# Four layer boundaries: the first tokens' x turned before the last late weight piece, and six late pieces in every one of the four stages

## The chip, the cores and the metric

The kernel runs on one core of a Trainium2 chip. The metric is device time in microseconds (us), median of several runs. Engines: TensorE (PE in the profile, its weight loads PEld), VectorE (DVE), ScalarE (ACT), GpSimd (POOL) and SyncE (SP, which issues the weight loads).

## What is computed

256 tokens of 1024 features go through a long chain of layers: a first block of depth two (gated feed-forwards, an mLSTM mixer, a differential attention, gated per-layer embeddings), a second block (attention beside a state-space mixer, then a product-key expert layer), and a third block (gated recurrence beside forgetting attention, then a feed-forward). Each sublayer begins by norming x and ends by adding its normed result to x. The four boundaries of this case lie between a projection and the next sublayer:

```python
h = swiglu(rms_norm(x, g[0]), w_ffn_in[layer, 0], w_ffn_out[layer, 0])   # f00, f10
x = x + 0.5 * rms_norm(h, g[1])
h = rms_norm(x, g[2])                                                     # boundary f00 -> ml
h = mlstm_mixer(h, ...)            # layer 0: ml; layer 1: df, diff_attention
x = x + rms_norm(h, g[3])
h = swiglu(rms_norm(x, g[4]), w_ffn_in[layer, 1], w_ffn_out[layer, 1])    # boundaries ml -> f01, df -> f11
...
x = x + rms_norm_3(mix_out, mix_norm_post[layer])
h = rms_norm_3(x, ffn_norm_pre[layer])                                    # boundary m3 -> f3
```

Everything is in fp32 accuracy: each weight and each activation is split in a high and a low half, and three of the four products are made.

## The kernel before

**Stages.** f00, ml, f01, p0, f10, df, f11, p1, m2, pr, m3 and f3 run in this order. Each ends in a `down` product, which is accumulated over weight pieces in four PSUM banks: two for the first 128 tokens (j = 0), two for the second (j = 1).

**Weight pieces.** SP loads chunks of 1 MB into three slots. ACT makes the high half of each piece of 128x1024 (`high_to`, L2589), DVE the low half (`low_to`, L1375). The halves live in a ring of four buffers, or aside in free parts of a large array (`ASIDE`, `FOLLOW`). A planner's loop in `Program` says how many pieces are made ahead (`upto`), and both engines make them in a fixed place of their own program. A load into a slot waits for the low halves of the chunk before in that slot.

**Late pieces.** `down` (L654) runs over KT pieces, 22 in a feed-forward and 8 in ml, df and m3. Most are used for both token halves at once, twelve matmuls of L622 each. The last `LATE[key]` pieces are kept: first all of them for j = 0 (six matmuls each), then all of them for j = 1, so that the first tokens' banks fill early. LATE is 6 for f00 and 5 for ml, df and m3.

**The boundary.** When its banks are full, `residual` (DVE L1434 weighting, L1447 sum, L1461 moment; ACT L2630 squares, L2637 squares of x; POOL L1265 the inverse root) gives the new x, and L2645 (ACT) and L1467 (DVE) its normed halves. TensorE turns it by transposes (`turn_half`, L505). ACT scales the eight turned tiles of a token half into the high part (L2614) and DVE makes the low part (L1413); the code calls both `enter`. Then `four` (L559, matmuls L573) makes the next stage's first four pieces, 24 matmuls for the first tokens, then the second turn, then 24 for the second tokens. Before the change the order on TensorE is: late pieces j = 0, late pieces j = 1, turn of j = 0, `four` for j = 0, turn of j = 1, `four` for j = 1. On ACT the squares of j = 1 come before `enter` of j = 0; on DVE all of the weighting and sum of j = 1 comes before it.

**df's down.** `before(t)` puts the end of the differential attention between its pieces on TensorE: heads' probabilities are turned (L855), the values' products made (L881 to L883), and the heads' outputs turned in pairs (L905). Pieces 0 and 1 run before the parts of t = 2, piece 2 runs between those and the parts of t = 3; pieces 3 to 7 are the late ones. On DVE and ACT the halves of the next pieces stand between the attention's parts too; the copy of a head's values is L1850, its norming L1863.

Of the kernel before, what the change touches and what calls it, by code (L numbers as in the profile page):

```python
# [298 lines left out]
class Program:  # L299
# [150 lines left out]
    def gb(self, slot):  # L450
# [11 lines left out]
LATE = {"f00": 6, "ml": 5, "f01": 5, "p0": 8, "f10": 5, "df": 5, "f11": 5, "p1": 8, "m2": 3, "pr": 4, "m3": 5, "f3": 3}  # L462
ASIDE = {"f00": (23552, 13312, 15360, 17408, 19456, 21504), "ml": (20608, 22656, 0, 4096, 6144),
# [8 lines left out]
          "pr": (4096, 6144), "m3": (10240, 22656)}  # L472
# [3 lines left out]
def tensor_engine(k):  # L476
# [177 lines left out]
    def down(key, KT, act, ready, ring=32, before=nothing):  # L654
# [15 lines left out]
        for j in range(2):  # L670
            for t, n, hi, lo in kept:
                ins = products(t, n, hi, lo, (j,))
                if j:
                    ins.then_inc(k.piece_read, 1)
            if j == 0:
                filled((key, "o", 0), ins)
            else:
                k.full[key, "o", 1] = k.piece_read, n + 1
# [52 lines left out]
    def ffn(key, prev, third=nothing):  # L731
        turn_half(key + ".x", prev, 0)
        second = lambda: turn_half(key + ".x", prev, 1)
        if key == "f00":
            second()
        gated(key, 22, turned_x(key + ".x"), None if key == "f00" else second, third)
        down(key, 22, k.pair(0, 22), hidden(key))
# [13 lines left out]
    def mlstm(prev):  # L751
        turn_half("ml.x", prev, 0)
# [71 lines left out]
        down("ml", 8, k.pair(14336, 8), out_halves("ml"))  # L824
# [33 lines left out]
    def diff(prev, kx, kv_ready):  # L858
# [72 lines left out]
        down("df", 8, k.pair(4096, 8), turned("df.o"), before=before)  # L931
# [217 lines left out]
    def mix3(prev):  # L1149
# [45 lines left out]
        down("m3", 8, k.pair(0, 8), out_halves("m3.o"))  # L1195

    def ffn3(prev):
        turn_half("f3.x", prev, 0)
# [4 lines left out]
    ffn("f00", "in")  # L1203
# [156 lines left out]
def vector_engine(k):  # L1360
# [57 lines left out]
    def residual(key, src, banks, row, factor, more, arrive, pre=nothing):  # L1418
# [4 lines left out]
        enter = into[key] if more else nothing  # L1423
# [58 lines left out]
        x_low(0)  # L1482
        if not banks:
# [19 lines left out]
        if not tokens_next:  # L1503
            if banks:
# [8 lines left out]
        if banks and not tokens_next:  # L1513
            enter(0, range(4, 8))
# [808 lines left out]
    def mix3(prev):  # L2323
# [106 lines left out]
        mg, tt, mx = k.ar(14336, 8, 256), k.ar(21632, 2, 2, 256), k.pair(0, 8)  # L2430
# [141 lines left out]
def scalar_engine(k):  # L2572
# [45 lines left out]
    def residual(key, src, banks, row, factor, more, arrive, pre=nothing, mid=nothing):  # L2618
# [37 lines left out]
        if banks:  # L2656
            x_high(0)
            square(1, 0)
            square(1, 1)
            mid(0)  # L2660
            enter(0)
# [539 lines left out]
    def mix3(prev):  # L3201
# [86 lines left out]
        tt, mx = k.ar(21632, 2, 2, 256), k.pair(0, 8)  # L3288
# [266 lines left out]
```

## Time and profile before

| | us |
|---|---|
| median of 3 runs | 2874.62 (2874.25 to 2874.62) |
| the profiled execution, device time | 2875.41 |
| its span from first to last instruction | 2873.6 |
| TensorE busy | 2818.5 (98%) |
| DVE busy | 1952.3 (68%) |
| ACT busy | 1636.2 (57%) |
| mean granted TensorE clock | 0.995 |

A matmul's time in the trace runs from its issue to its modelled end, and successive ones overlap, so a busy TensorE is not one at its peak. What counts at a boundary is the start of each group of instructions on each engine. A timeline line gives the start of a group, the time from its first start to its last end, the engine, the source line and operation, output and inputs, the count, and in brackets the idle time of the engine before it with what ended it.

### The profile page before, as it was taken

To read this page: it belongs to the slowest core of one execution; us is meant where nothing else is said; L and a number is where in the kernel's file an instruction comes from. 1 tells how busy PE (TensorE), PEld (TensorE's weight loads), DVE (VectorE), ACT (ScalarE), POOL (GpSimd) and SP (SyncE) were. 2 spreads that over 40 slices of the span, in tenths; PEclk is the share of its full clock that TensorE was granted. 3 is DMA by queue.
4 is the path that set the end of the run, shared out by engine and by line. 5 is a ranking of instruction groups with operands and counts; after the bars stand their busy time and mean duration, and the time that the engine had idled before them with its cause. 6 is when DMAs were issued, how large, how long until landed. Compare 5 with 4: busy or idle time off the path is not lost.

```text
span 2873.6 us, 44340 instructions
## 1 busy us (share of the span) xinstructions
PE 2818.5 (98%) x17826; PEld 2544.8 (89%) x17826; DVE 1952.3 (68%) x3367; ACT 1636.2 (57%) x2802; POOL 342.4 (12%) x310
## 2 busy tenths in 40 slices
PE   8999999999989999999999999999999999999999
PEld 7889888788978877899999999999888889999997
DVE  6657765676676667768864898677555566756775
ACT  5545654755655564556655445777454555755663
POOL 0000000000010002000001444896000000000000
PEclk9999999999999999999999999999999999999999
DMA  6654556456435555445365554334555564536454
GB/s 213 198 170 161 178 198 214 132 194 223 142 117 168 204 175 179 132 138 183 89 184 170 189 177 162 133 133 148 196 197 192 190 233 129 185 106 213 136 195 150
DMA packets 304539, 490.32 MB, mean 171 GB/s; under 512 B 10880, under 2 KB 236544, under 8 KB 295632
## 3 DMA queue, kind: packets, MB, share of 16 engines
q1 hardware_dynamic: 303200, 480.09, 50.6%
q0 software_dynamic: 1136, 7.41, 0.7%
q8 instruction: 142, 2.33, 0.3%
q14 instruction: 61, 0.50, 0.1%
HBM read 485.37 MB, written 2.10 MB: 170 GB/s over the span
## 4 chain that ended last, share of the span: by engine, by line
PE 89%; DVE 7%; ACT 2%; DMA 1%; issue 1%; POOL 0%; SPq 0%; DVEq 0%; POOLq 0%; ACTq 0%
PE ps L622 30%; PE ps L556 11%; PE ps L552 11%; PE ps L553 11%; PE ps L701 10%; PE ps L700 5%; PE ps L573 2%; PE ps L1130 2%; DVE halves L1375 2%; PE ps L1165 1%; PE ps L505 1%; DVE AR L2234 1%; DVE R L1375 1%; PE ps L855 0%; DMA raw<-in_w_ffn_in 0%
## 5 line engine op out<-in xcount | busy, mean ns | idle before, releaser
L2589 ACT ACTIVATE halves<-raw 128x1024 fp32r<-128x1024 f32 (+1 forms) x842 | 878.6, 1052 | 681.6 <-PE ps L622 330.7
L1375 DVE TENSOR_TENSOR halves<-raw,halves 128x1024 fp32r<-128x1024 f32 (+1 forms) x806 | 964.3, 1218 | 223.3 <-ACT halves L2589 220.6
L552 PE MATMUL ps<-XX,halves 128*128 128x256 f32 (+1 forms) x2360 | 586.7, 286 | 0.0
L553 PE MATMUL ps<-XX,halves 128*128 128x256 f32 (+1 forms) x2360 | 578.3, 283 | 0.0
L622 PE MATMUL ps<-halves,XX 128*128 128x512 f32 x2256 | 525.0, 393 | 5.5 <-DVE XX L1413 2.8
L622 PEld LDWEIGHTS ps<-halves,XX 128*128 128x128 f32 x2256 | 424.4, 189 | 96.9 <-DVE XX L1413 5.2
L552 PEld LDWEIGHTS ps<-XX,halves 128*128 128x128 f32 (+1 forms) x2360 | 451.5, 191 | 0.8
L553 PEld LDWEIGHTS ps<-XX,halves 128*128 128x128 f32 (+1 forms) x2360 | 452.0, 192 | 0.3
L556 PE MATMUL ps<-XX,halves 128*128 128x256 f32 (+1 forms) x2360 | 331.5, 283 | 0.7 <-DVE halves L1375 0.7
L622 PE MATMUL ps<-halves,R 128*128 128x512 f32 x1404 | 322.3, 391 | 0.0
L701 PE MATMUL ps<-XX,halves 128*128 128x512 f32 x1264 | 317.8, 393 | 2.2 <-DVE XX L1413 2.2
L622 PEld LDWEIGHTS ps<-halves,R 128*128 128x128 f32 x1404 | 264.3, 189 | 54.6
L556 PEld LDWEIGHTS ps<-XX,halves 128*128 128x128 f32 (+1 forms) x2360 | 304.3, 192 | 1.2 <-DVE halves L1375 1.1
L701 PEld LDWEIGHTS ps<-XX,halves 128*128 128x128 f32 x1264 | 227.4, 189 | 43.1 <-issue 2.5
L1265 POOL TENSOR_TENSOR st<-st 128x1 f32<-128x1 f32 x44 | 27.9, 635 | 1507.7 <-DVE st L1440 1305.7
L700 PEld LDWEIGHTS ps<-XX,halves 128*128 128x128 f32 x1264 | 172.4, 190 | 13.5 <-issue 1.3
L700 PE MATMUL ps<-XX,halves 128*128 128x256 f32 x1264 | 176.3, 282 | 1.0 <-DVE halves L1375 1.0
L1390 DVE TENSOR_TENSOR XX<-AR,XX 128x256 fp32r<-128x256 f32 x128 | 54.2, 425 | 142.8 <-ACT XX L3194 142.8
L1345 POOL TENSOR_SCALAR raw<-iota,xsel 128x128 f32<-128x128 f32 x128 | 136.7, 1074 | 37.5 <-PE ps L1130 23.2
L1596 DVE TENSOR_TENSOR AR<-AR,ps 128x256 f32<-128x256 f32 x164 | 68.6, 421 | 83.1 <-ACT AR L2755 83.1
L2755 ACT ACTIVATE AR<-ps 128x256 f32<-128x256 f32 x164 | 61.3, 376 | 88.7 <-PE ps L701 88.7
L1270 POOL TENSOR_TENSOR halves<-raw,halves 128x1024 fp32r<-128x1024 f32 x36 | 91.5, 2540 | 157.6 <-ACT halves L2589 157.6
(365 smaller groups left out, 3505.1 us busy)
## 6 DMA issues: line engine op xcount, KB each, us to landing
raw<-in_w_ffn_in SPq DMA_DIRECT2D x88, 1024.0 KB, 5.1
raw<-in_w_in SPq DMA_DIRECT2D x74, 1024.0 KB, 5.3
raw<-in_uT SPq DMA_DIRECT2D x64, 1024.0 KB, 4.9
raw<-in_peer_v SPq DMA_DIRECT2D x64, 1024.0 KB, 4.9
raw<-in_w_ffn_out SPq DMA_DIRECT2D x44, 1024.0 KB, 4.9
raw<-in_w_up SPq DMA_DIRECT2D x24, 1024.0 KB, 5.8
raw<-in_mlstm_w_in SPq DMA_DIRECT2D x12, 1024.0 KB, 5.4
raw<-in_w_down SPq DMA_DIRECT2D x12, 1024.0 KB, 4.9
```

The source lines that it names most:

```text
L552: mm(o[:, ts], hi[:, q, 0:M], xh[:, k0 + q, ts], start=first and q == 0, stop=False)
L553: mm(o[:, ts], hi[:, q, 0:M], xl[:, k0 + q, ts], start=False, stop=False)
L556: ins = mm(o[:, ts], lo[:, q, 0:M], xh[:, k0 + q, ts], start=False, stop=last and q == a - 1)
L622: ins = mm(ps[:, bs[j * (width // 512) + h], :], xv[:, k0 + t, j * 128:(j + 1) * 128], wv[:, t, h * 512:(h + 1) * 512], start=first and q ...
L700: mm(o[:, 0:256], lo[:, p, :], X[0][:, p, :], start=False, stop=False)
L701: ins = mm(o.rearrange("p (h t) -> p h t", t=256), hi[:, q, :], k.XX[:, :, q, :], start=q == 0, stop=q == 7)
L1270: nc.gpsimd.tensor_tensor(lo, src, hi.bitcast(F32), ALU.subtract).then_inc(k.lo_pool, 1)
L1345: nc.gpsimd.tensor_scalar(OA[:, g % 2, q, :], k.iota[:], ih1[:, 4 * g + q:4 * g + q + 1], gw[:, 4 * g + q:4 * g + q + 1], ALU.is_equal, AL ...
L1375: te.tensor_tensor(lo, src, hi.bitcast(F32), ALU.subtract).then_inc(k.lo_made, 1)
L1596: te.tensor_tensor(dst, dst, o[:, 0:256], ALU.add) \
L2589: act(hi, src, ACT.Copy).then_inc(k.hi_made, 1)
L2755: act((sg if a_ == "g" else hb)[:, f // 2 % 2, g, :], ps[:, k.wide_banks(f).of(tile), 256:512], ACT.Copy) \
```

## The change

- `ml`, `df` and `m3` get a sixth late piece, with a place aside for it; m3's last places move, and m3's scratch tile `tt` moves to make room.
- For f00, ml, df and m3 (`TURNED_EARLY`) the turn of the first tokens' x is issued inside `down`, before the last late piece of j = 1, and no longer at the start of the next stage.
- On ACT `enter` of the first tokens (all eight tiles) comes before the second tokens' squares. On DVE its tiles 0 to 3 come before the second tokens' weighting, tiles 4 to 7 after their sum and before their moment.

```diff
-LATE = {"f00": 6, "ml": 5, "f01": 5, "p0": 8, "f10": 5, "df": 5, "f11": 5, "p1": 8, "m2": 3, "pr": 4, "m3": 5, "f3": 3}
+LATE = {"f00": 6, "ml": 6, "f01": 5, "p0": 8, "f10": 5, "df": 6, "f11": 5, "p1": 8, "m2": 3, "pr": 4, "m3": 6, "f3": 3}
-ASIDE = {..., "ml": (20608, 22656, 0, 4096, 6144),
+ASIDE = {..., "ml": (20608, 22656, 0, 4096, 6144, 11264),
-         "f10": (13312, 20480, 22528, 24576, 0), "df": (13312, 15360, 17408, 24576, 0),
+         "f10": (13312, 20480, 22528, 24576, 0), "df": (13312, 15360, 17408, 24576, 0, 19456),
-         "pr": (0, 2048, 4096, 6144), "m3": (4096, 6144, 8192, 10240, 22656)}
+         "pr": (0, 2048, 4096, 6144), "m3": (4096, 6144, 8192, 10240, 22528, 24576)}
+TURNED_EARLY = ("f00", "ml", "df", "m3")
...
     def down(key, KT, act, ready, ring=32, before=nothing, turn_next=nothing):
...
         for j in range(2):
             for t, n, hi, lo in kept:
+                if j and t == KT - 1:
+                    turn_next()
                 ins = products(t, n, hi, lo, (j,))
...
-        turn_half(key + ".x", prev, 0)
+        if prev not in TURNED_EARLY:
+            turn_half(key + ".x", prev, 0)
...
-        down("ml", 8, k.pair(14336, 8), out_halves("ml"))
+        down("ml", 8, k.pair(14336, 8), out_halves("ml"), turn_next=lambda: turn_half("f01.x", "ml", 0))
...
@@ vector_engine, residual
         x_low(0)
+        if key in TURNED_EARLY:
+            enter(0, range(4))
...
         if not tokens_next:
-            if banks:
+            if key in TURNED_EARLY:
+                enter(0, range(4, 8))
+            elif banks:
                 enter(0, range(4))
...
-        if banks and not tokens_next:
+        if banks and not tokens_next and key not in TURNED_EARLY:
             enter(0, range(4, 8))
...
@@ mix3
-        mg, tt, mx = k.ar(14336, 8, 256), k.ar(21632, 2, 2, 256), k.pair(0, 8)
+        mg, tt, mx = k.ar(14336, 8, 256), k.ar(16384, 2, 2, 256), k.pair(0, 8)
...
@@ scalar_engine, residual
             x_high(0)
+            if key in TURNED_EARLY:
+                enter(0)
             square(1, 0)
             square(1, 1)
             mid(0)
-            enter(0)
+            if key not in TURNED_EARLY:
+                enter(0)
```

The downs of f00, df and m3 get their `turn_next` in the same way, and the turns at the start of ml and f3 are taken out.

## Rows read from the trace of the kernel before

**Rows 1.** The page, chain that ended last: shares of the span by engine.

```profile
PE 89%; DVE 7%; ACT 2%; DMA 1%; issue 1%; POOL 0%; SPq 0%; DVEq 0%; POOLq 0%; ACTq 0%
```

**Rows 2.** Timeline, boundary f00: start us, us, engine, line, operation, xcount, idle before.

```profile
197.77 0.72 ACT L2645 ACTIVATE AR<-AR,st 128x512 f32<-128x512 f32 x1 [0.91 <-POOL st L1265]
...
200.33 1.03 PE L505 MATMUL ps<-ident,AR 128*128 128x128 f32 x8
...
200.53 1.41 DVE L1434 TENSOR_TENSOR AR<-ps,AR 128x512 f32<-128x512 f32 x2 [2.27 <-PE ps L622]
...
202.35 5.85 PE L573 MATMUL ps<-halves,XX 128*128 128x512 f32 x24 [0.98 <-ACT XX L2614]
...
206.13 0.73 ACT L2645 ACTIVATE AR<-AR,st 128x512 f32<-128x512 f32 x1 [0.91 <-POOL st L1265]
...
208.04 1.03 PE L505 MATMUL ps<-ident,AR 128*128 128x128 f32 x8
```

**Rows 3.** Timeline, boundary ml.

```profile
299.82 13.31 PE L622 MATMUL ps<-R,R 128*128 128x512 f32 x58
...
305.37 2.36 DVE L1375 TENSOR_TENSOR halves<-raw,halves 128x1024 fp32r<-128x1024 f32 x2 [1.09 <-ACT halves L2589]
...
307.65 1.28 DVE L1434 TENSOR_TENSOR AR<-ps,AR 128x512 f32<-128x512 f32 x2
...
313.06 0.72 ACT L2645 ACTIVATE AR<-AR,st 128x512 f32<-128x512 f32 x1 [0.92 <-POOL st L1265]
...
313.93 1.06 PE L505 MATMUL ps<-ident,AR 128*128 128x128 f32 x8 [0.80 <-ACT AR L2645]
...
321.05 1.03 PE L505 MATMUL ps<-ident,AR 128*128 128x128 f32 x8
```

**Rows 4.** Timeline, boundary m3.

```profile
2651.85 2.36 DVE L1375 TENSOR_TENSOR halves<-raw,halves 128x1024 fp32r<-128x1024 f32 x2 [0.73 <-ACT halves L2589]
...
2654.13 1.28 DVE L1434 TENSOR_TENSOR AR<-ps,AR 128x512 f32<-128x512 f32 x2
...
2659.53 0.72 ACT L2645 ACTIVATE AR<-AR,st 128x512 f32<-128x512 f32 x1 [0.91 <-POOL st L1265]
...
2660.40 1.06 PE L505 MATMUL ps<-ident,AR 128*128 128x128 f32 x8 [0.57 <-ACT AR L2645]
...
2667.50 1.03 PE L505 MATMUL ps<-ident,AR 128*128 128x128 f32 x8
```

**Rows 5.** Timeline, boundary df.

```profile
849.84 1.41 DVE L1434 TENSOR_TENSOR AR<-ps,AR 128x512 f32<-128x512 f32 x2 [2.81 <-PE ps L622]
...
855.26 0.73 ACT L2645 ACTIVATE AR<-AR,st 128x512 f32<-128x512 f32 x1 [0.92 <-POOL st L1265]
...
856.45 1.03 PE L505 MATMUL ps<-ident,AR 128*128 128x128 f32 x8
...
864.20 1.03 PE L505 MATMUL ps<-ident,AR 128*128 128x128 f32 x8
864.84 2.17 ACT L2614 ACTIVATE XX<-ps,cols 128x128 fp32r<-128x128 f32 x8 [1.87 <-PE ps L505]
...
866.01 2.16 DVE L1413 SCALAR_TENSOR_TENSOR XX<-ps,cols,XX 128x128 fp32r<-128x128 f32 x8 [3.00 <-ACT XX L2614]
```

**Rows 6.** Timeline of TensorE, the end of df's attention.

```profile
827.44 4.39 PE L622 MATMUL ps<-halves,R 128*128 128x512 f32 x12
...
840.25 0.69 PE L905 MATMUL ps<-ident,AR 128*128 128x128 f32 x2 [7.31 <-DVE AR L1863]
```

**Rows 7.** Chain of work that ended last, same stretch: start us, us, what.

```profile
831.35 5.06 DMA raw<-in_w_ffn_in
...
838.74 0.34 DVE AR L1850
```

**Rows 8.** Stretches: us, busy PE, PEld, DVE, ACT, POOL (x), PEclk, DMA share, GB/s.

```profile
540.30:543.70 3.40, 1.70 (x6) 0.75 (x5) 2.61 (x8) 2.00 (x5) 0.55 (x1) 1.00 0.55 188
543.70:547.10 3.40, 3.24 (x12) 2.96 (x13) 0.91 (x4) 2.19 (x10) 0.00 (x0) 0.50 0.00 0
...
840.60:844.00 3.40, 3.18 (x10) 2.37 (x10) 2.52 (x7) 2.12 (x4) 0.18 (x1) 0.50 0.33 103
```

More of the change, by code:

```diff
@@ L460 @@
               "pr": 128, "m3": 8, "f3": 24}
-LATE = {"f00": 6, "ml": 5, "f01": 5, "p0": 8, "f10": 5, "df": 5, "f11": 5, "p1": 8, "m2": 3, "pr": 4, "m3": 5, "f3": 3}
-ASIDE = {"f00": (23552, 13312, 15360, 17408, 19456, 21504), "ml": (20608, 22656, 0, 4096, 6144),
+LATE = {"f00": 6, "ml": 6, "f01": 5, "p0": 8, "f10": 5, "df": 6, "f11": 5, "p1": 8, "m2": 3, "pr": 4, "m3": 6, "f3": 3}
+ASIDE = {"f00": (23552, 13312, 15360, 17408, 19456, 21504), "ml": (20608, 22656, 0, 4096, 6144, 11264),
          "f01": (14848, 16896, 18944, 20992, 23040), "p0": (16384, 18432, 20480, 22528),
[1 row of a table removed]
[1 row of a table added]
          "f11": (14848, 16896, 18944, 20992, 23040), "p1": (16384, 18432, 20480, 22528),
          "m2": (0, 12288, 23552),
[1 row of a table removed]
[1 row of a table added]
+TURNED_EARLY = ("f00", "ml", "df", "m3")
 FOLLOW = {"f00": (15360, 21504), "ml": (20608, 22656), "p0": (16384, 18432), "df": (15360, 17408), "m2": (0, 12288),
-          "pr": (4096, 6144), "m3": (10240, 22656)}
+          "pr": (4096, 6144), "m3": (10240, 22528)}
 FACTOR = {"f00": 0.5, "f01": 0.5, "f10": 0.5, "f11": 0.5}
@@ L652, in tokens, with down @@
                 k.full[key, s0, j] = k.piece_read, n + 1
-    def down(key, KT, act, ready, ring=32, before=nothing):
+    def down(key, KT, act, ready, ring=32, before=nothing, turn_next=nothing):
         bs = [aux.take(pe, (key, "o", i)) for i in range(4)]
@@ L729, in out_halves, with ffn @@
         return lambda t: [s["out_lo"].need((key, t - t % 2))]
-    def ffn(key, prev, third=nothing):
-        turn_half(key + ".x", prev, 0)
+    def ffn(key, prev, third=nothing, turn_next=nothing):
+        if prev not in TURNED_EARLY:
+            turn_half(key + ".x", prev, 0)
         second = lambda: turn_half(key + ".x", prev, 1)
@@ L736, in ffn @@
         gated(key, 22, turned_x(key + ".x"), None if key == "f00" else second, third)
-        down(key, 22, k.pair(0, 22), hidden(key))
+        down(key, 22, k.pair(0, 22), hidden(key), turn_next=turn_next)
     def turn_kv(_):
@@ L751, in mlstm @@
     def mlstm(prev):
-        turn_half("ml.x", prev, 0)
         rx = turned_x("ml.x")
@@ L929, in before @@
                 out_pair(6)
-        down("df", 8, k.pair(4096, 8), turned("df.o"), before=before)
+        down("df", 8, k.pair(4096, 8), turned("df.o"), before=before, turn_next=lambda: turn_half("f11.x", "df", 0))
     def attend(key, score, vv, yt, E_, dT, value_need, expd):
@@ L1194, in mix3 @@
         features("m3.pb", 8, k.pair(17536, 8), lambda c: [aux.gone(("m3", "y", c - c % 2))])
-        down("m3", 8, k.pair(0, 8), out_halves("m3.o"))
+        down("m3", 8, k.pair(0, 8), out_halves("m3.o"), turn_next=lambda: turn_half("f3.x", "m3", 0))
     def ffn3(prev):
-        turn_half("f3.x", prev, 0)
         gated("f3", 24, turned_x("f3.x"), lambda: turn_half("f3.x", prev, 1))
@@ L1202, in tensor_engine @@
     pe.wait_ge(*s["vec"].need("constants"))
-    ffn("f00", "in")
+    ffn("f00", "in", turn_next=lambda: turn_half("ml.x", "f00", 0))
     mlstm("f00")
@@ L3287, in mix3 @@
         yT, E_ = k.pair(17536, 8), k.ar(23680, 2, 384)
-        tt, mx = k.ar(21632, 2, 2, 256), k.pair(0, 8)
+        tt, mx = k.ar(16384, 2, 2, 256), k.pair(0, 8)
         gt = (k.ar(2048, 8, 256), k.ar(12288, 8, 256))
```

## The prediction, made before the change was run

> **What bounds the kernel now.** I read the page's chain of work first, then the timeline of the four boundaries that the diff touches. TensorE is the bound: 89% of the chain is its own work [rows 1], so time is won or lost only where TensorE stands idle or is delayed. At a boundary the reader should see three things: when TensorE finishes the down product, when the first tokens' x is normed (L2645, ACT), and when the second tokens' x is turned (the second run of L505). The second is the new wait to watch, because TensorE goes on only when both turns are done.
>
> At f00 the first turn runs 200.33, the four pieces' first half (L573) starts at 202.35 after 0.98 idle, and the second turn starts at 208.04 although the second x was normed at 206.13 + 0.73 = 206.86 [rows 2]. So there is 1.18 us of slack in the second tokens' tail. At ml the run of L622 ends at 299.82 + 13.31 = 313.13, the first turn waits until 313.93 for L2645, and the second is at 321.05 [rows 3]. m3 is the same picture (2660.40 and 2667.50) [rows 4]. At df the first turn waits for nothing (x normed at 855.99, turn at 856.45), the second is at 864.20 [rows 5].
>
> **The change, in units.** One matmul of L622 takes (13.31 - 0.39) / 57 = 0.227 us from start to start (58 in 13.31, each 0.39 long) [rows 3]. A late piece has six for each token half: 1.36 us. Eight turning transposes take 1.03 us in all, and the next matmul can follow after 0.87 (1.03 less the overlap of the last, seven steps of about 0.11) [rows 2].
>
> **Part 1, the turn moved ahead of the last late piece.** It wants to start 1.36 us before the old end of L622. Call its start T. Then the last piece runs T + 0.87 to T + 2.23, and the four pieces' first half follows at once: ACT takes the eight turned tiles from T + 0.64 to T + 2.81 (864.84 - 864.20, and 2.17 long) [rows 5], just ahead of TensorE. The idle 0.98 before L573 is gone. That is the gain, about 1.1 us where T isn't late.
>
> **Part 2, the second tokens' tail.** Their banks are full at T + 2.4, but ACT takes their squares only after the eight tiles, T + 2.8, and DVE starts their weighting after four low halves: it can begin at T + 1.81 (866.01 - 864.20), four of the eight take about 1.12, less 0.08 of overlap with the next: T + 2.85 [rows 5]. From the weighting to the second norm it is 206.13 - 200.53 = 5.60 [rows 2], then 0.73 for the norm and 0.15 to the turn (313.06 + 0.72 = 313.78, turn at 313.93) [rows 3]. Second turn: T + 2.85 + 5.60 + 0.73 + 0.15 = **T + 9.33**. TensorE has reached it at T + 2.23 + 24 x 0.227 = T + 7.7, so a new wait of 1.6 us takes the place of the old gap. For df's first tokens, with nothing beside them, the same stretch took 855.26 - 849.84 = 5.42 [rows 5]; that is the lower bound, T + 9.15, and I keep 5.60, since four low halves still sit between the sum and the moment on DVE. Queued behind the waiting turn on TensorE: the other token half, then everything. Nothing hides it.
>
> **Part 3, the sixth late piece and whether T is late.** T is the later of "old end less 1.36" and "x normed plus 0.15".
> - f00 has six late pieces already. The wanted T is 200.33 - 1.36 = 198.97, x is normed at 197.77 + 0.72 = 198.49 [rows 2]. T = 198.97, second turn 208.30 against 208.04: **+0.26**.
> - ml: the wanted T is 313.13 - 1.36 = 311.77. The sixth late piece fills the first tokens' banks 1.36 earlier, at 305.0 instead of 306.3. But DVE is making low halves of the next four weight pieces until 305.37 + 2.36 = 307.73 and starts the weighting at 307.65 [rows 3]; these come at the arrival of weights, in DVE's program order, and the diff leaves the order alone: by the planner's loop the pieces made ahead at each late piece are the same from the eighth last on. So x is normed at 313.78 as before, and T stays 313.93, 2.16 us after TensorE wants it. Second turn 323.26 against 321.05: **+2.21**.
> - m3: weighting at 2654.13, at the end of the same kind of low halves; T stays 2660.40; second turn 2669.73 against 2667.50: **+2.23** [rows 4].
> - df: the weighting starts with the full banks (849.84), so T = 856.45 - 1.36 = 855.09 does move with them; 864.42 against 864.20: **+0.22** [rows 5].
>
> **Part 4, df's third piece.** With five late pieces, piece 2's twelve matmuls stand between the attention's last parts: 4.39 us from 827.44 [rows 6]. After them TensorE waits 7.31 us, until 840.25, for head 6 and 7. That wait is not TensorE's doing: the chain goes through a weight load from 831.35 to 836.41, its halves, and then the copy of head 7's values at 838.74 [rows 7], which ACT and DVE have queued behind the halves of the next pieces. With six late pieces the twelve matmuls leave this cover. The wait grows and ends at the same time; the twelve come after it: 12 x 0.227 = **+2.72**. Bounds: 0 if the load came correspondingly sooner, 4.39 if they ran at the half clock throughout. The clock is 0.50 just after 840.60 [rows 8] in any case, so the work that follows loses the same there; I take 2.72.
>
> The tiles' new places (tt, the sixth aside piece) cost nothing that a row shows: no instruction is added. No DMA is moved; SP's loads wait for low halves, which don't move before the norms.
>
> **Sum.** 0.26 + 2.21 + 0.22 + 2.23 + 2.72 = **7.6 us**. The profiled execution took 2875.41 (span 2873.6) and would take 2883.0; it is 0.8 above the median of 2874.62, which becomes **2882.2**. About 0.2%, or 5.7 us, is what a measurement of this kernel can tell from no change.
>
> **Clock.** A stretch in which TensorE was busy 1.70 of 3.40 us was followed by one at 0.50, which is 1.2 GHz [rows 8]. The new waits at ml and m3 (2.16 and 1.93, then 1.6) are of that size, so the half clock may follow. If it falls on the four pieces' first half it costs 1.7 and the second wait of 1.6 hides nearly all; if it falls later it costs up to 1.7 a boundary. The Trainium skill (TensorE: Matmul & The Clock Gate, HAM oscillation) makes trouble only of idle gaps longer than these; by it this is 0, by the row up to 3.4 for the two. I leave it out of the sum and keep it in the range.
>
> The Trainium skill (ScalarE: Activation LUTs, What ACT_TABLE_LOAD costs) gives by its formula an estimate of 0.29 us for each of ACT's eight back-to-back tiles; row 864.84 has 0.27. By the page the tail would be some 0.2 us longer at each boundary, 8.4 in all instead of 7.6.
>
> **Rivals.**
> 1. *The first norm follows the banks* (faster side of slower). If ml's and m3's weighting starts 1.36 sooner, T does too: 7.6 - 2 x 1.36 = 4.9, **2879.5**. For it: the chain really starts from full banks at f00 and df. Against it: 307.65 touches the end of L1375 [rows 3]. The same time comes out if df's load comes sooner by the twelve matmuls (7.6 - 2.7). 17%.
> 2. *It works as meant: faster.* One mechanism: both token halves' x are ready when TensorE wants them, so each boundary gives back its idle time before L573: 1.1 at f00 and df, 1.3 at ml, 1.1 at m3, sum 4.6, **2870.0**. It decides at T + 7.7: the second tail would have to be 1.6 us shorter than its row, T on time at ml and m3, and df's twelve matmuls free. 9%.
> 3. *Half clock beyond the cover* at ml, m3 or after df's longer wait: 2 x 1.7 more, **2885.6**. 12%.
> 4. The forecast, 2880.5 to 2884: 62%.
>
> **Range and chances.** The range takes in the forecast, rival 1 and most of rival 3 down to the tail's lower bound: 2878.0 to 2886.0; outside are rival 2 and the ends. Slower by over 0.2% needs 2880.4: forecast nearly whole and rival 3, 0.68; within 0.2%: rival 1 and the forecast's lower end, 0.23; faster 0.09.
>
> **What would show it.** f00: no idle before L573, second turn near 9.3 after the first with an idle of about 1.6 before it. ml and m3: 2 us idle before the first turn, with six matmuls of L622 behind it, and L1434 starting still at the end of L1375. df: the wait before L905 grows from 7.3 to about 10 and ends on the same load; 72 matmuls of late pieces after it instead of 60. Wrong if at ml L1434 starts with the first tokens' banks, if the tail from the first to the second turn is under 8 us, or if L905's wait ends sooner.

## The result and the profile after

| | before | after |
|---|---|---|
| median of 12 runs each, us | 2873.78 (2871.08 to 2875.45) | 2880.15 (2876.90 to 2884.95) |
| the profiled execution, device time | 2875.41 | 2878.57 |
| its span | 2873.6 | 2876.8 |
| mean granted TensorE clock | 0.995 | 0.995 |

The ratio is 1.0026, with an interval of 1.0018 to 1.0034: 0.0026 x 2873.78 = 7.5 us slower (5.2 to 9.8); the medians differ by 6.4. The change makes the kernel slower, by about what was forecast (7.6). One execution of late_only, an experiment below, took 3973.31 us at a mean granted clock of 0.654 and is in no ratio.

Two words are used throughout. The *tail* of a boundary is the time from the start of the first tokens' turn to the start of the second tokens' turn. A load's *landing* is the moment at which ACT, idle until then for this load, starts on it.

Line numbers of after lie 1 to 6 higher: L505 is L506, L573 is L574, L622 is L623, L905 is L908, L1375 is L1377, L1434 is L1436, L1863 is L1869, L2589 is L2595, L2614 is L2620, L2645 is L2651. I read the four boundaries first, as before.

**f00**, timeline of after: start us, us, engine, line, operation, xcount, idle before.

```profile
198.98 1.03 PE L506 MATMUL ps<-ident,AR 128*128 128x128 f32 x8
199.62 2.18 ACT L2620 ACTIVATE XX<-ps,cols 128x128 fp32r<-128x128 f32 x8 [1.11 <-PE ps L506]
199.77 1.63 PE L623 MATMUL ps<-R,R 128*128 128x512 f32 x6
...
201.24 5.91 PE L574 MATMUL ps<-halves,XX 128*128 128x512 f32 x24
201.84 1.28 DVE L1436 TENSOR_TENSOR AR<-ps,AR 128x512 f32<-128x512 f32 x2
```

The turn starts at 198.98, the six matmuls of the last late piece follow it, and the four pieces start 2.26 us after the turn with no idle: the 0.98 before L573 in [rows 2] is gone, as the change means it. What it gets in return stands in the weighting of the second tokens, 201.84, which is 2.86 behind the turn, and in the second turn at 208.25 (208.04 before).

**ml and m3**, two stretches of the timeline of after:

```profile
303.79 2.01 ACT L2595 ACTIVATE halves<-raw 128x1024 fp32r<-128x1024 f32 x2 [1.00 <-DMA raw<-in_w_ffn_in]
304.89 2.36 DVE L1377 TENSOR_TENSOR halves<-raw,halves 128x1024 fp32r<-128x1024 f32 x2 [0.65 <-ACT halves L2595]
...
307.17 1.28 DVE L1436 TENSOR_TENSOR AR<-ps,AR 128x512 f32<-128x512 f32 x2
...
313.45 1.06 PE L506 MATMUL ps<-ident,AR 128*128 128x128 f32 x8 [0.38 <-ACT AR L2651]
...
322.75 1.06 PE L506 MATMUL ps<-ident,AR 128*128 128x128 f32 x8 [1.09 <-ACT AR L2651]
...
2651.65 2.01 ACT L2595 ACTIVATE halves<-raw 128x1024 fp32r<-128x1024 f32 x2 [2.42 <-DMA raw<-in_w_up]
...
2655.02 1.28 DVE L1436 TENSOR_TENSOR AR<-ps,AR 128x512 f32<-128x512 f32 x2
...
2661.30 1.06 PE L506 MATMUL ps<-ident,AR 128*128 128x128 f32 x8 [1.66 <-ACT AR L2651]
...
2670.60 1.06 PE L506 MATMUL ps<-ident,AR 128*128 128x128 f32 x8 [1.10 <-ACT AR L2651]
```

The second turn is 9.30 behind the first in both (7.12 and 7.10 in [rows 3, 4]), and TensorE waits for the norm of the second tokens' x, where before the norm was done when TensorE came to it. The weighting still starts at the end of the low halves of L1377 (304.89 + 2.36 = 307.25).

**df**, timeline of TensorE in after:

```profile
841.12 0.69 PE L908 MATMUL ps<-ident,AR 128*128 128x128 f32 x2 [9.05 <-DVE AR L1869]
...
842.54 17.44 PE L623 MATMUL ps<-R,R 128*128 128x512 f32 x66
...
859.82 1.04 PE L506 MATMUL ps<-ident,AR 128*128 128x128 f32 x8
...
869.10 1.06 PE L506 MATMUL ps<-ident,AR 128*128 128x128 f32 x8 [1.10 <-ACT AR L2651]
```

The wait before heads 6 and 7 is 9.05 us (7.31 in [rows 6]), and now 66 matmuls follow it before the turn. What ends it is a weight load, in the chain of work that ended last: start us, us, what.

```profile
832.25 5.03 DMA raw<-in_w_ffn_in
...
837.30 1.07 ACT halves L2595
...
838.39 1.23 DVE halves L1377
839.62 0.34 DVE AR L1856
```

It is the chain of [rows 7], link by link. The link ahead of the load is a low half on DVE (L1377, 831.09 and 1.14 long; 830.19 and 1.15 in before): it frees the slot, and the load is issued. So the end of the wait hangs on DVE's order as well as on the 5.03 us of the transfer.

**The four boundaries in one table.** From the first matmul of `down` to the second turn, in us, each worked out from two starts in the timeline; the same for every kernel of the experiments, so that what differs elsewhere between two executions is kept out. The last column has the tails:

| kernel | f00 | ml | df | m3 | sum | first to second turn |
|---|---|---|---|---|---|---|
| before | 67.57 | 29.95 | 48.09 | 29.61 | 175.2 | 7.70, 7.12, 7.76, 7.10 |
| after | 67.77 | 31.40 | 52.10 | 33.14 | 184.4 | 9.27, 9.30, 9.28, 9.30 |
| df_five_late | 67.78 | 33.00 | 49.23 | 33.05 | 183.1 | 9.27 to 9.31 |
| late_only | 67.60 | 30.65 | 50.77 | 30.85 | 179.9 | 7.74, 7.18, 7.76, 7.31 |
| turn_only | 67.78 | 31.38 | 49.74 | 31.81 | 180.7 | 9.27 to 9.31 |
| old_order_act_dve | 68.51 | 33.44 | 52.13 | 33.57 | 187.6 | 9.99 to 10.02 |
| lazy_late_waits | 67.78 | 31.54 | 52.24 | 32.35 | 183.9 | |
| early_norm_changed | 67.78 | 32.45 | 51.96 | 32.68 | 184.9 | 9.27, 10.21, 9.27, 10.21 |
| fill_df_wait | 67.57 | 29.61 | 46.66 | 31.16 | 175.0 | 7.70, 7.55, 7.74, 7.10 |
| fill_df_wait_early_norm | 67.61 | 29.76 | 46.22 | 30.74 | 174.3 | ml 7.88, m3 8.19 |
| fill_df_wait_more | 67.59 | 29.61 | 44.63 | 30.07 | 171.9 | ml 7.52, m3 7.10 |

After has 9.2 us more than before at the boundaries, but its profiled execution is only 3.2 longer. The other 6 lie elsewhere, and nothing in the traces ties them to the change: in the execution of before TensorE ran at half clock in stretches of 3.4 us near 543.7 [rows 8], 1079.6 and 1089.8 and for 6.8 us near 1386.8, 17.1 in all; in that of after for 3.4 us near 1093.0. Half of the difference, 6.8, is the most that this can be worth. So one execution of each can't be compared by its end; the boundaries can, and so can 12 runs.

### The profile page after: what moved, and what is told of

It is laid out like the page before. It is cut to its first block, busy times and chain, and to the rows that moved or that the text cites. A ratio compares the mean times of both kernels' runs of the same rounds, so it can differ in the third digit from the quotient of the medians.

```text
span 2876.8 us, 44338 instructions
## 1 busy us (share of the span) xinstructions
PE 2814.6 (98%) x17826; PEld 2539.8 (88%) x17826; DVE 1951.7 (68%) x3367; ACT 1637.6 (57%) x2802; POOL 342.4 (12%) x310
## 4 chain that ended last, share of the span: by engine, by line
PE 88%; DVE 7%; ACT 2%; DMA 1%; issue 1%; POOL 1%; SPq 0%; DVEq 0%; POOLq 0%; ACTq 0%
PE ps L623 30%; PE ps L557 11%; PE ps L553 11%; PE ps L554 11%; PE ps L704 10%; PE ps L703 5%; PE ps L1133 2%; DVE halves L1377 2%; PE ps L574 2%; PE ps L1168 1%; DVE XX L1415 1%; PE ps L506 1%; DVE R L1377 1%; POOL st L1267 1%; DVE AR L2240 1%
## 5 line engine op out<-in xcount | busy, mean ns | idle before, releaser
L2595 ACT ACTIVATE halves<-raw 128x1024 fp32r<-128x1024 f32 (+1 forms) x839 | 875.5, 1052 | 678.4 <-PE ps L623 329.5
L1377 DVE TENSOR_TENSOR halves<-raw,halves 128x1024 fp32r<-128x1024 f32 (+1 forms) x803 | 960.7, 1217 | 222.7 <-ACT halves L2595 219.6
L623 PE MATMUL ps<-halves,XX 128*128 128x512 f32 x2256 | 522.5, 392 | 5.5 <-DVE XX L1415 2.9
L623 PEld LDWEIGHTS ps<-halves,XX 128*128 128x128 f32 x2256 | 422.5, 188 | 96.1 <-DVE XX L1415 5.2
L623 PE MATMUL ps<-halves,R 128*128 128x512 f32 x1368 | 312.5, 389 | 0.0
L623 PEld LDWEIGHTS ps<-halves,R 128*128 128x128 f32 x1368 | 256.4, 188 | 53.0
L623 PE MATMUL ps<-R,R 128*128 128x512 f32 x504 | 119.1, 396 | 2.1 <-ACT R L2595 2.1
L623 PEld LDWEIGHTS ps<-R,R 128*128 128x128 f32 x504 | 95.7, 191 | 22.8 <-ACT R L2595 2.9
```

The source lines that it names most:

```text
L623: ins = mm(ps[:, bs[j * (width // 512) + h], :], xv[:, k0 + t, j * 128:(j + 1) * 128], wv[:, t, h * 512:(h + 1) * 512], start=first and q ...
L1377: te.tensor_tensor(lo, src, hi.bitcast(F32), ALU.subtract).then_inc(k.lo_made, 1)
L2595: act(hi, src, ACT.Copy).then_inc(k.hi_made, 1)
```

## The experiments

Two questions. Which of the two parts costs what: the turn with its order, or the sixth late piece? And was each term's reason the one given? The theory is the forecast's: the second tokens' tail of 9.3 (against 7.1 at ml and m3), and df's twelve matmuls out of the cover of a wait whose end is fixed. The rival theories are that the first norm follows the banks (so that the sixth piece gives something back at ml and m3), and that the turn alone would be a gain.

**df_five_late.** After, with df's sixth late piece undone.

```diff
-LATE = {..., "df": 6, ...}
+LATE = {..., "df": 5, ...}
-"df": (13312, 15360, 17408, 24576, 0, 19456)
+"df": (13312, 15360, 17408, 24576, 0)
```

> The changed kernel, but with df's five late pieces back (piece 2's twelve matmuls again between the attention's last parts). Theory A (piece 2 was free cover for a wait that ends on a weight load): TensorE's wait before head 6 and 7 is turned goes from 9.05 us back to about 7.3 us and ends on the same load; the run of late pieces after it is 60 matmuls, not 72; df gives back 2.7 us and up to 1.7 of half clock, so 2.7 to 4.4 us less than the changed kernel. But its first norm then comes 1.1 us after TensorE wants the turn, so the second turn is about 1.3 us later than in the kernel before at df. Against the kernel before: +3.5 to +5. Theory B (the early turn is what costs at df): no more than 1 us against the changed kernel.

Measured: 2878.75, ratio to before 1.0023 (1.0015 to 1.0032), that is +6.6. (The expectation added its own terms wrongly: 0.26, 2.2, 1.3 and 2.2 make 6.0, not 3.5 to 5.) At df it gave back 52.10 - 49.23 = 2.9, for an expected 2.7, and the wait shrank to what twelve matmuls, partly at half clock, leave of it. Two more things are in this 2.9: the norm came 0.89 after the turn's place (second row below), and less of the late run stood at half clock than in after. By the times it gave back only 7.5 - 6.6 = 0.9, with intervals that overlap nearly whole, so the 2.9 is the trace's and not shown by the times. TensorE in df_five_late:

```profile
843.26 0.69 PE L908 MATMUL ps<-ident,AR 128*128 128x128 f32 x2 [7.36 <-DVE AR L1869]
...
858.97 1.06 PE L506 MATMUL ps<-ident,AR 128*128 128x128 f32 x8 [0.89 <-ACT AR L2651]
```

ml, which this edit doesn't touch, took 33.00 instead of 31.40. That led to the reading of the loads below.

**late_only.** Before, with six late pieces and their places, and the old turn and order.

```diff
-LATE = {... "ml": 5, ... "df": 5, ... "m3": 5, ...}
+LATE = {... "ml": 6, ... "df": 6, ... "m3": 6, ...}
```

(with the diff's ASIDE, FOLLOW and `tt`)

> The kernel before with six late pieces in ml, df and m3 (and the new places), but each first turn where it was and the old order on ACT and DVE. Theory A: df alone costs 2.7 to 4.4 us; ml nothing (TensorE waits for the last late pieces' high halves, 0.8 us, but waited for the norm anyway); m3 0.8 us, because its 1.3 us wait for the high halves ends the late run after the norm. Sum +3.5 to +5. Theory B (early turn costs, late pieces are free): within 1 us of the kernel before.

Measured: 2874.77, ratio 1.0011 (1.0003 to 1.0020), that is +3.2, for an expected 3.5 to 5. The boundaries give +4.7, of which df is +2.68: the twelve matmuls (2.72). The run of late matmuls after the wait is 72 long. TensorE in late_only:

```profile
840.12 0.69 PE L905 MATMUL ps<-ident,AR 128*128 128x128 f32 x2 [9.02 <-DVE AR L1863]
...
841.54 17.68 PE L622 MATMUL ps<-R,R 128*128 128x512 f32 x72
```

At ml and m3 the sixth piece gives nothing back: +0.70 and +1.24, where the rival wanted the banks' 1.36 earlier norm to show. What is new there is a wait inside the run, for high halves. It does not end the late run after the norm, as was expected of m3 (TensorE still waits 0.27 for the norm there):

```profile
2642.47 16.58 PE L622 MATMUL ps<-R,R 128*128 128x512 f32 x72 [1.06 <-ACT R L2589]
```

**turn_only.** After, with LATE, ASIDE, FOLLOW and `tt` as before: the early turn and the new order alone.

```diff
-LATE = {... "ml": 6, ... "df": 6, ... "m3": 6, ...}
+LATE = {... "ml": 5, ... "df": 5, ... "m3": 5, ...}
```

> The kernel before with the four first turns ahead of the last late piece and the new order on ACT and DVE, but five late pieces in ml, df and m3. Theory A: from first to second turn 9.3 us at every boundary, so f00 +0.2, ml +2.2, m3 +2.2 (first turns at the time of the norm, as before), df +1.3 (its norm comes 1.1 us late for the wanted turn); sum +6. No 0.8 and 1.3 us waits of L622-type products for high halves at ml and m3, the wait at df 7.3 us. Theory B (the sixth piece is what costs, the early turn gives back the idle second before the four pieces): faster than the kernel before by 3 to 4 us.

Measured: 2876.86, ratio 1.0015 (1.0007 to 1.0024), boundaries +5.5: 0.21, 1.43, 1.65 and 2.20. The turn alone loses at every one of the four; the theory by which it is a gain is refuted. df costs more than the forecast's 0.22, which was for six late pieces (the expectation here had 1.3), for two reasons. The norm comes 0.89 after the turn's place, and TensorE's run of 30 matmuls before the banks took 8.65 us (842.46 to the weighting at 851.11) where before took 841.56 to 849.84, 8.28. Here piece 2 ran at full clock, and the wait grew by what that saved:

```profile
828.09 3.02 PE L623 MATMUL ps<-halves,R 128*128 128x512 f32 x12
...
841.14 0.69 PE L908 MATMUL ps<-ident,AR 128*128 128x128 f32 x2 [8.93 <-DVE AR L1869]
```

4.39 + 7.31 = 11.70 in [rows 6], 3.02 + 8.93 = 11.95 here; without the piece, in after, it is 9.05, since there other work of TensorE ahead of the wait took longer (part 4 below). Counted from the start of df's product, the end of the wait stands at 24.14 (before), 24.12 (after), 24.09 (late_only), 24.17 (turn_only) and 24.22 (df_five_late), and between 24.17 and 24.44 in the other six kernels. The wait is a remainder up to a nearly fixed end, whichever of these orders TensorE has ahead of it. That is the strongest number for the forecast's largest term.

**old_order_act_dve.** After, with ACT's and DVE's order as before: only TensorE turns early.

```diff
 (vector_engine, residual)
-        if key in TURNED_EARLY:
-            enter(0, range(4))
...
-            if key in TURNED_EARLY:
-                enter(0, range(4, 8))
-            elif banks:
+            if banks:
                 enter(0, range(4))
...
-        if banks and not tokens_next and key not in TURNED_EARLY:
+        if banks and not tokens_next:
             enter(0, range(4, 8))
 (scalar_engine, residual)
-            if key in TURNED_EARLY:
-                enter(0)
             square(1, 0)
...
-            if key not in TURNED_EARLY:
-                enter(0)
+            enter(0)
```

> The changed kernel's TensorE order with the old order on ACT and DVE: the first tokens' eight turned tiles are taken after the second tokens' squares (ACT) and sum (DVE). Theory A (the second tokens' tail is the new bound, and taking the tiles first delays it by only 0.4 us): the squares start at the bank's filling, but the four pieces' first half starts 4.3 us after the first turn instead of 2.2 and paces with ACT, so the second turn comes about 9.9 us after the first, 0.6 later than in the changed kernel at each boundary: +2 to +3 us against it. Theory B (the delayed squares are what costs): second turn 9.0 us or less after the first, 1 us or more below the changed kernel.

Measured: 2886.09 (5 runs), ratio 1.0049 (1.0036 to 1.0062). The tail from first to second turn is 10.0 at all four boundaries, forecast 9.9. Timeline of f00:

```profile
201.37 1.03 PE L506 MATMUL ps<-ident,AR 128*128 128x128 f32 x8
...
203.83 1.41 DVE L1436 TENSOR_TENSOR AR<-ps,AR 128x512 f32<-128x512 f32 x2 [3.17 <-PE ps L623]
205.14 2.16 ACT L2616 ACTIVATE XX<-ps,cols 128x128 fp32r<-128x128 f32 x8
205.64 5.90 PE L574 MATMUL ps<-halves,XX 128*128 128x512 f32 x24 [1.85 <-ACT XX L2616]
```

The second tokens' weighting comes earlier (2.46 after the turn, not 2.86), but `enter` of the first waits behind the squares, and the four pieces start 4.27 after the turn instead of 2.26. So the change's new order on ACT and DVE isn't the fault; without it the early turn is worse. Both orders lose; my reading is that one of the two token halves must be second on ACT and DVE. The distance in time to after (2886.09 - 2880.15, about 6) is more than the four tails of 0.7; the two intervals are too wide for me to settle the rest.

**lazy_late_waits** (one execution). After, but TensorE waits for each late piece's halves only where it uses them, except in df.

```diff
             before(t)
+            if key != "df" and t >= KT - LATE[key]:
+                kept.append((t, None, None, None))
+                continue
             n, hi, lo = weights()
...
+                if n is None:
+                    n, hi, lo = weights()
```

> The changed kernel, but outside df TensorE waits for each late piece's high half when it uses it, not for all of them before the first. Theory A: the waits of 0.8 us (ml) and 1.3 us (m3) in the late run vanish, and nothing is gained, since the first turn still waits for the norm: waits before it grow by the same, second turns where they are in the changed kernel within what the arrival of weights varies (1.5 us). Theory B (those waits cost): from down to second turn 0.8 less at ml and 1.3 less at m3.

This is for a wait that the forecast did not have. `down` takes the halves of all late pieces before it uses the first. With six of them TensorE gets there with twelve matmuls less done, and stands: 0.77 at ml, and 1.34 at m3. m3 in after:

```profile
2644.44 15.20 PE L623 MATMUL ps<-R,R 128*128 128x512 f32 x66 [1.34 <-ACT R L2595]
```

In lazy_late_waits these waits are gone, and the one before the first turn has grown from 0.38 to 1.57 and from 1.66 to 2.46:

```profile
297.06 15.12 PE L623 MATMUL ps<-R,R 128*128 128x512 f32 x66
313.75 1.06 PE L506 MATMUL ps<-ident,AR 128*128 128x128 f32 x8 [1.57 <-ACT AR L2657]
...
2643.64 15.12 PE L623 MATMUL ps<-R,R 128*128 128x512 f32 x66
2661.22 1.06 PE L506 MATMUL ps<-ident,AR 128*128 128x128 f32 x8 [2.46 <-ACT AR L2657]
```

ml took 31.54 (31.40 in after) and m3 32.35 (33.14, with its load 0.8 later). TensorE loses nothing by the new wait itself, since what sets the turn is elsewhere.

**What sets the first norm at ml and m3.** ACT starts the high halves of the third of the next four pieces when its load has landed (303.79 at ml above, idle until then for a DMA). From there to the weighting it is 307.17 - 303.79 = 3.38 at ml and 2655.02 - 2651.65 = 3.37 at m3. It is 3.37 to 3.38 in before (304.28 to 307.65 [rows 3]), in df_five_late, in late_only and in turn_only as well, with five or with six late pieces. From the weighting to the turn it is 6.27 to 6.29 in each of these. ACT at ml in before:

```profile
304.28 2.01 ACT L2589 ACTIVATE halves<-raw 128x1024 fp32r<-128x1024 f32 x2 [1.44 <-DMA raw<-in_w_ffn_in]
```

So the first turn stands 9.65 behind a landing, and the landing moves from trace to trace: counted from the start of `down`, ml and m3, it was

| | ml | m3 |
|---|---|---|
| before | 13.18 | 12.87 |
| after | 12.45 | 14.18 |
| df_five_late | 14.04 | 14.11 |
| late_only | 13.82 | 13.89 |
| turn_only | 12.42 | 12.86 |
| old_order_act_dve | 13.76 | 13.90 |
| lazy_late_waits | 12.59 | 13.39 |
| early_norm_changed | 13.73 | 13.95 |
| fill_df_wait | 12.41 | 14.40 |
| fill_df_wait_early_norm | 12.66 | 14.04 |
| fill_df_wait_more | 12.44 | 13.32 |

With that, after's two boundaries come out: ml 12.45 - 13.18 + (9.30 - 7.12) = +1.45, measured +1.45; m3 14.18 - 12.87 + (9.30 - 7.10) = +3.51, measured +3.53. late_only's +0.70 and +1.24 are the same two landings (13.82 - 13.18, 13.89 - 12.87) and 0.06 and 0.21 of tail. ml of df_five_late, with its 33.00, is the same sum:

```profile
306.07 2.01 ACT L2595 ACTIVATE halves<-raw 128x1024 fp32r<-128x1024 f32 x2 [2.43 <-DMA raw<-in_w_ffn_in]
...
309.44 1.28 DVE L1436 TENSOR_TENSOR AR<-ps,AR 128x512 f32<-128x512 f32 x2
...
315.73 1.06 PE L506 MATMUL ps<-ident,AR 128*128 128x128 f32 x8 [1.98 <-ACT AR L2651]
```

What moves the landing was not tested, but the table and the traces say something of it. The load is issued at the same place in all eleven traces, 6.6 us after the start of `down` at ml and 6.8 at m3, so what varies is its time in flight. In nine of the 22 boundaries a packet of 16 KB, of a DMA queue that the profile calls "instruction", starts in that flight, 8.7 to 9.1 us after the start of `down`, and all nine landed at 13.7 to 14.2. At the other 13 this packet comes at 2.9 to 4.3 us, and eleven of them landed at 12.4 to 13.4; m3 of fill_df_wait and of fill_df_wait_early_norm landed late all the same, so the packet is not the whole of it. A line of the view of DMA queues (packets, MB, share) for m3 in after, from 2644 to 2649 us; in before the same stretch has none:

```profile
q8 instruction: 1, 0.02, 1.7%
```

All nine lie at stages with six late pieces, of which there are twelve; none lies at the ten with five. The mean landing is 13.65 with six and 13.06 with five, and the two ranges overlap. So the sixth piece may cost some 0.6 us at each of ml and m3 in this roundabout way; the traces can neither show nor exclude it.

**early_norm_changed** (one execution). After, with the last low half of the next four pieces on DVE made no longer before the first norm at ml and m3. DVE then makes it at the next place in its program where low halves stand, behind the weighting of the second tokens.

```diff
-        low_to(k.upto[v.cur - 1])
+        if key not in ("ml", "m3"):
+            low_to(k.upto[v.cur - 1])
         residual(
```

> The changed kernel, but at ml and m3 DVE makes the last of the next four low halves after the second tokens' variance. Theory A: first turn 1.1 us earlier at m3, where TensorE waits 1.7 for it, and 0.4 at ml, where it waits 0.4; the second tail grows by up to 0.4. From down to second turn 0.7 less at m3 and 0 to 0.4 less at ml. Theory B (the norm waits for the banks or for ACT): no change.

Measured: 2884.06. The weighting starts 2.23 after the landing instead of 3.37, so the low half was what stood between. But the moved piece now stands in the second tail. Timeline of ml:

```profile
318.38 1.98 PE L574 MATMUL ps<-halves,XX 128*128 128x512 f32 x8
...
320.54 1.22 DVE L1377 TENSOR_TENSOR halves<-raw,halves 128x1024 fp32r<-128x1024 f32 x1
320.71 1.46 POOL L1267 TENSOR_TENSOR st<-st 128x1 f32<-128x1 f32 x1 [5.51 <-DVE st L1442]
...
321.90 3.88 PE L574 MATMUL ps<-halves,XX 128*128 128x512 f32 x16 [1.54 <-DVE halves L1377]
```

The four pieces wait 1.54 in their middle for that low half, and POOL's inverse root took 1.46 beside it (0.55 otherwise). The tail is 10.21: the first norm wins 1.14 and the second turn loses 0.91 of it (at most 0.4 was expected). Counted from the landing, ml takes 32.45 - 13.73 = 18.72 where after takes 31.40 - 12.45 = 18.95.

**fill_df_wait.** Before, without any part of the change: in df the j = 0 half of late pieces 3, 4 and 5 runs ahead of the turn of heads 6 and 7, so inside the wait; DVE and ACT take the copy-out of heads 4 and 5 one place sooner.

```diff
                 kept.append((t, n, hi, lo))
+                if key == "df" and t < 6:
+                    products(t, n, hi, lo, (0,))
         for j in range(2):
             for t, n, hi, lo in kept:
+                if j == 0 and key == "df" and t < 6:
+                    continue
...
                 out_pair(4)
+            if t == 6:
                 out_pair(6)
... (vector_engine and scalar_engine)
         def before(t):
+            if t == 2:
+                out_pair(4)
...
                 if i == 10:
-                    out_pair(4)
                     out_pair(6)
```

> The kernel before, with one thing moved at df: the first tokens' half of late pieces 3, 4 and 5 (18 matmuls) runs on TensorE before the turn of heads 6 and 7, and heads 4 and 5 are taken on ACT and DVE before the halves of the next pieces. Theory A (the wait before heads 6 and 7 ends on a weight load whatever TensorE does, so work put there is free): the wait shrinks by 18 x 0.227 = 4.1 us and ends at the same time; from the start of df's down product to the second turn 44.0 us instead of 48.1; with less idle the half clock after the wait may go, up to 1.7 us more. -4 to -6 us against the kernel before. Theory B (the operands aren't there in time): at most 1.4 us.

Measured: 2867.49 against 2872.14, ratio 0.9982 (0.9973 to 0.9991), that is 5.2 us (2.6 to 7.8) faster than before. It is the forecast's reasoning turned round: if twelve matmuls taken out of the cover cost 2.7, work put into it should be won. TensorE in fill_df_wait:

```profile
831.93 1.63 PE L622 MATMUL ps<-R,R 128*128 128x512 f32 x6
834.48 3.00 PE L622 MATMUL ps<-R,R 128*128 128x512 f32 x12 [0.92 <-DVE R L1891]
839.77 0.69 PE L909 MATMUL ps<-ident,AR 128*128 128x128 f32 x2 [2.29 <-DVE AR L1868]
...
842.90 11.51 PE L622 MATMUL ps<-R,R 128*128 128x512 f32 x42 [1.54 <-DVE R L1891]
```

The 18 matmuls lie in what was one wait of 7.31, and the wait still ends on the load. They are worth 18 x 0.227 = 4.1 us, and 44.0 was expected for df; but df gave only 48.09 - 46.66 = 1.4 in this profile. The last row shows where most of the rest is: only pieces 6 and 7 are left for j = 0, they need the copied-out heads 6 and 7, and TensorE now waits 1.54 for them. From the second turn of heads to the next matmul it is 842.90 - 840.68 = 2.22, against 841.56 - 841.16 = 0.40 in before: 1.8 lost. The load took 5.36 us instead of 5.06 and the wait ended 0.3 later, and half clock (6.8 us, as in before) cost 0.55 more of the late run.

So df in this profile does not account for the 5.2 us. Part of them is clock away from df: the mean granted clock was 0.997 to 0.998 in the eleven executions and 0.995 to 0.997 in the 21 of before, and the 6.8 us at 0.50 near 1386.8 in before are not in this trace. How much of the gain is the moved work alone isn't shown more closely.

**fill_df_wait_more.** The same, and piece 3's j = 1 half (six matmuls) between the turn of heads 6 and 7 and piece 6, where that 1.54 was.

```diff
+                elif key == "df" and t == 6:
+                    products(*kept[0], (1,)).then_inc(k.piece_read, 1)
         for j in range(2):
             for t, n, hi, lo in kept:
-                if j == 0 and key == "df" and t < 6:
+                if key == "df" and (t < 6 if j == 0 else t == 3):
                     continue
```

> fill_df_wait, and one more piece of work moved: the second tokens' half of late piece 3 (six matmuls) runs between the turn of heads 6 and 7 and piece 6, where fill_df_wait waits 1.54 us for DVE's low halves of these heads. Theory A (that wait too is fixed from outside TensorE): the wait falls to about 0.2, the late run after it ends 1.4 us sooner, but the first norm, 6.3 us after the banks, ends it 0.5 to 0.9 later than that, so the second turn comes 0.5 to 0.9 us sooner than in fill_df_wait. Theory B (TensorE's order shifts the wait with it): no change. By time the two can hardly be told apart.

Measured: 2866.99 against 2871.97, ratio 0.9985 (0.9976 to 0.9994); with fill_df_wait at 0.9982 the two can't be told apart in time. In the profile the 1.54 is gone and df takes 44.63, 2.0 less than fill_df_wait, for an expected 0.5 to 0.9; some of that is the clock, at half for 3.4 instead of 6.8 us. TensorE in fill_df_wait_more:

```profile
841.38 11.21 PE L622 MATMUL ps<-R,R 128*128 128x512 f32 x42
...
853.48 1.07 PE L505 MATMUL ps<-ident,AR 128*128 128x128 f32 x8 [0.89 <-ACT AR L2653]
```

The next wait, 0.89 for the first norm, is already there.

**fill_df_wait_early_norm.** fill_df_wait, with the same low half taken from before the first norm at ml and m3, but put right behind it, ahead of the second tokens' weighting.

```diff
         x_low(0)
+        if key in ("ml", "m3"):
+            low_to(k.next_four(key))
...
-        low_to(k.upto[v.cur - 1])
+        if key not in ("ml", "m3"):
+            low_to(k.upto[v.cur - 1])
```

> The same, and at ml and m3 DVE makes the last of the next four low halves after the first tokens' norm, not before it. Theory A (the norm at ml and m3 starts with the end of DVE's low halves): L1434-type weighting starts 1.1 us earlier against the start of down, TensorE's wait before the first turn (0.8 and 0.6) goes, second turn 0.8 and 0.6 earlier: -1.4 us against fill_df_wait. Theory B (the norm waits for the banks): no change.

Measured: 2870.67, ratio 0.9989 (0.9980 to 0.9998); the further 1.4 us didn't come. The turn came sooner after the landing and the four pieces then waited. m3:

```profile
2651.69 1.06 PE L505 MATMUL ps<-ident,AR 128*128 128x128 f32 x8 [0.61 <-ACT AR L2654]
...
2654.18 5.87 PE L573 MATMUL ps<-halves,XX 128*128 128x512 f32 x24 [1.42 <-ACT XX L2623]
```

The tails are 7.88 and 8.19 instead of fill_df_wait's 7.55 and 7.10. Wherever the low half was put, most of what the first norm won came back in the tail.

## Why the prediction was right, and where it wasn't

- **Part 1, the turn.** Right: no idle before L574 at f00, the four pieces 2.26 after the turn (forecast 2.23). ACT's tiles came somewhat faster than in either of the forecast's readings: eight in 2.18 and seven in 1.92 put them 0.25 apart. The forecast's 0.27 is the 2.17 divided by eight, with the length of the last tile in it, and its other estimate, 0.29 each and 8.4 us in all, did not come.
- **Part 2, the tail of the second tokens.** Forecast T + 9.33, measured 9.27 to 9.31 at twelve boundaries of three kernels (after, df_five_late, turn_only). Of its terms, the weighting was to start at T + 2.85 and did at T + 2.86. In old_order_act_dve, worked out in the same manner, 9.9 became 10.0. Reading it as a chain over ACT, DVE and POOL, and not from TensorE's wait, is what made the number good. The wait itself shows as 1.09 to 1.10, not 1.6: the profile counts it from the modelled end of the last matmul, and the 24 took 5.91, with 0.36 of waiting for DVE's last four tiles in their weight loads.
- **Part 3, T at f00.** +0.26, measured +0.20.
- **Part 3, T at ml and m3.** Forecast unmoved; +2.21 and +2.23. The tail moved by 2.18 and 2.20, and the start of the weighting held its 3.37 from the landing, so the mechanism is right and rival 1, by which the norm follows the banks, is refuted for these two. But the step took the landing of the load as fixed, from one row; it moves by up to 2 us, hence +1.45 and +3.53 in this pair of profiles. Their sum, 4.98, is near the forecast 4.44 because one was early and one late, which is luck. Whether the sixth piece itself makes the landing later, by the 0.6 of the means above, stays open.
- **Missing from part 3:** the new waits of 0.77 and 1.34 for all six pieces' high halves. They cost nothing, as lazy_late_waits shows, but a sum without a later turn would have had to pay for them. With the moved landings they are why the sign that the forecast named, 2 us of idle before the first turn, came as 0.38 and 1.66. The diff's larger LATE means "wait for more, sooner"; I had read it only as "fill the banks sooner".
- **Part 3, T at df.** +0.22 in the tail by the forecast; in the trace its tail is 9.28 against 7.76, with the turn wanted 1.36 sooner: 0.16. Right.
- **Part 4, df's piece 2.** +2.72; late_only, in which nothing else changes at df, gives +2.68; df_five_late gives 2.9 back, with the two other things in it. The wait ended 24.1 to 24.4 us after the start of `down` in every kernel. "From 7.3 to about 10" for the wait was high: 9.05. The 4.39 of piece 2 don't all turn into waiting, since in after the attention's own small matmuls before the wait ran at half clock too (the 0.50 begins at 826.7) and TensorE stood 0.43 among them for a copy on DVE.
- **The clock, left out of the sum.** After's df is 52.10 - 48.09 = 4.01 over before, 1.07 more than 2.72 + 0.22. This is rival 3, at df. Stretches of after (us, busy PE, PEld, DVE, ACT, POOL, clock, DMA share, GB/s):

```profile
840.60:844.00 3.40, 2.66 (x8) 1.93 (x9) 2.19 (x8) 2.05 (x6) 0.69 (x1) 0.50 0.63 198
844.00:847.20 3.20, 3.20 (x9) 2.52 (x8) 3.20 (x5) 1.49 (x2) 0.00 (x0) 0.50 0.11 27
```

and the second of them in before:

```profile
844.00:847.20 3.20, 3.20 (x16) 2.64 (x15) 3.03 (x3) 0.62 (x1) 0.00 (x0) 0.99 0.38 99
```

Nine matmuls instead of sixteen in the same time. From the first late matmul to full banks, after took 853.22 - 842.54 = 10.68 for 36 matmuls, 2.5 over 36 x 0.227; before took 8.28 for 30, 1.5 over; late_only, with the same longer wait as after, 851.08 - 841.54 = 9.54 for 36, 1.4 over. The stretch at half clock reached 4.7 us into the late run in after and 2.3 in late_only. So the longer wait alone doesn't bring the longer half clock. But lazy_late_waits and early_norm_changed, which have after's program at df, show it too: 20.5 us at 0.50, 4.6 and 4.3 into the late run, df at 52.24 and 51.96. So all three traces of this program at df have a term of about 1 us that the sum left out, and it may be a standing part of the change's price there; three traces can't settle it. At ml and m3 the waits of 0.4 to 1.7 were followed by no stretch at 0.50 in after. The Trainium skill (TensorE: Matmul & The Clock Gate, HAM oscillation) warns of idle gaps longer than these; in after the boundaries ml and m3 agree with it. [rows 8] don't: a stretch with 1.70 us of work in 3.40, with one gap of 0.86 us in it and one of 1.01 at its end, was followed by 0.50.
- **Rival 2** (works as meant) needed the second tail 1.6 us shorter. turn_only shows it is not.

The likeliest sum, 7.6, against 7.5 by the ratio and 6.4 by the medians, is closer than its terms deserve: the profile pair has 9.2 at the boundaries. With the landings of before in place of its own, after would have 9.2 - (14.18 - 12.87) - (12.45 - 13.18) = 8.6, an estimate, near the 8.7 that the forecast's 7.6 and the clock's 1.1 make. The interval of the ratio, 5.2 to 9.8, takes in all of these, so the times can't choose between them.

## What to carry to other kernels

Giving one half of the work its engines first only helps where the other half has slack: count the second half's chain over the vector engines before you move the first. A long wait on a fixed end (a load) is cover. Work taken out of it cost its full time here (2.68 of 2.72); work put into it is won as far as its operands are there (1.4 of 4.1 at df at the first try, where TensorE then stood for the next operands), and a kernel with it ran at 0.9982 of before. Where a boundary hangs on a load's landing, compare distances from that landing between two traces, not the starts themselves.

## What the hardware showed that I had not expected

- The landing of the same weight load, counted from the start of the same stage, lay between 12.4 and 14.4 us in these traces, though it was issued at the same place. All nine landings with a 16 KB packet of the instruction queue in their flight were at 13.7 or later; that the one causes the other was not tested.
- The length of a stretch at half clock (0.50, 1.2 GHz) around the same df wait was 17.1 us in late_only and 20.5 in after, while before had two separate ones, 3.4 and 6.8. TensorE stood for 7.3 to 9.05 in each. Such stretches elsewhere (1386.8 for 6.8 us in before, none there in after) differ between traces, and can put a comparison of two profiles by their ends off by some 6 us.
- POOL's 128x1 operation of the inverse root took 1.46 us beside DVE's low half (two inputs from SBUF, the on-chip memory) and 0.55 to 0.56 without it. It is so in every trace: of the 44 such operations in before, four took 1.46, and these four are the ones that ran beside a low half; in early_norm_changed, which puts two more beside one, it is six. The Trainium skill (GPSIMD Engine Reference, Key points) says that GpSimd shares its SBUF interfaces with VectorE and contends with instructions of two SBUF inputs; the row agrees.
